# Turning round the operands of the state-space chunk products in a hybrid trunk kernel

## The reference

```
u = xc.reshape(B, L, 32, 16)
bu = einsum('blgc,gpc->blgp', u, b_bar)
states = scan(state_t = lam_bar * state_{t-1} + bu_t)
y = einsum('blgp,gcp->blgc', states, c).real + d_skip * u
y = gelu(y);  y = y * sigmoid(y @ glu_w + glu_b)
```

## Time and profile before

| | us |
|---|---|
| median of three runs | 1096.8 |
| profiled execution, time | 1097.05 |
| profiled execution, span | 1095.2 |
| PE busy | 915.2 (84% of the span) |
| PEld busy | 629.7 (57%) |
| DVE busy | 331.4 (30%) |
| ACT busy | 193.6 (18%) |
| POOL busy | 222.1 (20%) |
| mean granted TensorE clock | 0.91 |

### The profile page before, as it was taken

The page is one execution under the profiler, slowest core; times in us unless marked ns, Lnnn a source line. Parts: engine busy times, 40 slices in busy tenths (PEclk is TensorE's granted clock), DMA queues, the critical chain, the costliest instruction groups (busy, mean ns, idle before and its releaser), DMA issues.

```text
span 1095.2 us, 14939 instructions
## 1 busy us (share of the span) xinstructions
PE 915.2 (84%) x5341; PEld 629.7 (57%) x5342; DVE 331.4 (30%) x591; ACT 193.6 (18%) x282; POOL 222.1 (20%) x247
## 2 busy tenths in 40 slices
PE   3999898999999999984989878676995997787870
PEld 2788577888887688873555444433553554444430
DVE  2793995570042444445111101000110110010015
ACT  4523125130143223230000000000000000000002
POOL 3457970430110000011111110101201111111100
PEclk9999699985799999995999999987998999999895
DMA  8593120520343585220799999629997999999965
GB/s 240 107 180 97 39 77 20 105 94 0 83 148 97 185 335 180 88 80 19 294 405 411 395 398 402 274 61 402 406 386 282 407 395 398 412 405 408 407 252 234
DMA packets 80886, 263.02 MB, mean 240 GB/s; under 512 B 33323, under 2 KB 34347, under 8 KB 72130
## 3 DMA queue, kind: packets, MB, share of 16 engines
q1 hardware_dynamic: 74450, 252.00, 62.2%
q0 software_dynamic: 6256, 10.51, 2.8%
q10 hardware_dynamic: 144, 0.02, 0.0%
HBM read 256.07 MB, written 15.47 MB: 248 GB/s over the span
## 4 chain that ended last, share of the span: by engine, by line
PE 59%; DMA 26%; POOL 5%; DVE 4%; issue 2%; ACT 2%; SPq 1%; DVEq 0%; POOLq 0%; ACTq 0%
PE ps L911 27%; PE ps L422 13%; DMA au<-in_exp_w_up 13%; DMA ssm<-in_exp_w_up 8%; PE ps L435 7%; DMA pair<-h_scratch,idx_now 2%; DMA choice_rows<-pair,put_now 2%; PE ps L896 2%; PE ps L414 2%; PE ps L1014 2%; PE ps L1013 2%; POOL w_lo L1657 2%; POOL ssm L1667 2%; PE ps L1015 1%; PE ps L888 1%
## 5 line engine op out<-in xcount | busy, mean ns | idle before, releaser
L422 PE MATMUL ps<-ssm,pair 128*64 128x256 f32 x1696 | 196.3, 387 | 28.5 <-DMA ssm<-in_exp_w_gate 11.7
L422 PEld LDWEIGHTS ps<-ssm,pair 128*64 128x64 f32 x1696 | 124.1, 139 | 109.7 <-issue 31.6
L584 DVE TENSOR_TENSOR pair<-pair,ps 128x256 f32<-128x256 f32 x32 | 13.5, 421 | 404.2 <-PE ps L422 404.2
L911 PE MATMUL ps<-h_hi,w_hi 128*128 128x512 f32 x288 | 115.8, 402 | 7.9 <-POOL w_lo L1657 6.3
L911 PE MATMUL ps<-h_lo,w_hi 128*128 128x512 f32 x288 | 114.2, 397 | 0.0
L911 PE MATMUL ps<-h_hi,w_lo 128*128 128x512 f32 x288 | 114.1, 396 | 0.0
L1657 POOL TENSOR_TENSOR w_lo<-raw,w_hi 128x1024 fp32r<-128x1024 f32 x34 | 87.2, 2570 | 132.2 <-ACT w_hi L1089 131.9
L1089 ACT CAST w_hi<-raw 128x1024 fp32r<-128x1024 f32 x60 | 62.8, 1049 | 223.1 <-PE ps L911 222.6
L435 PE MATMUL ps<-ssm,pair 128*64 128x512 f32 x288 | 72.6, 650 | 17.6 <-DVE pair L593 12.2
L435 PE MATMUL ps<-hl,pair 128*64 128x512 f32 x272 | 69.6, 658 | 15.7 <-DVE pair L593 11.6
L650 ACT COPY late<-ps 128x512 f32<-128x512 f32 x32 | 18.8, 586 | 356.5 <-PE ps L435 356.5
(11 more groups left out here) (277 smaller groups left out, 1167.8 us busy)
## 6 DMA issues: line engine op xcount, KB each, us to landing
ssm<-in_exp_w_gate SPq DMA_DIRECT2D x32, 2048.0 KB
au<-in_exp_w_up SPq DMA_DIRECT2D x16, 2048.0 KB
ssm<-in_exp_w_up SPq DMA_DIRECT2D x16, 2048.0 KB
ssm<-in_exp_w_down SPq DMA_DIRECT2D x16, 2048.0 KB, 20.7
hl<-in_exp_w_down SPq DMA_DIRECT2D x16, 2048.0 KB, 23.0
raw<-in_w_in SPq DMA_DIRECT2D x40, 512.0 KB, 4.0
raw<-in_w_branch SPq DMA_DIRECT2D x12, 512.0 KB, 3.7
raw<-in_w_out SPq DMA_DIRECT2D x8, 512.0 KB, 8.1
```

Of the source, the lines that this page charges most:

```text
L422: t = nc.tensor.matmul(ps[CAP * h:CAP * (h + 1), bank, 0:HALF], xgT[b][:, k], w[:, k, HALF * h:HALF * (h + 1)], start=k == 0, stop=k == KD ...
L911: t = nc.tensor.matmul(bank, lhs, rhs, start=k == 0 and n == 0, stop=k == 2 * count - 1 and n == 2)
```

## The change

The chunk products exchange their operands. Now `u8v` and the states are stationary (64 columns: the chunks), and taps and carries move (128 columns: 8 tokens x 16 channels). The result has chunks on the partitions. Group q goes to partitions 0 to 63 and group q + 16 to partitions 64 to 127 of the same bank, and the two alternate in program order; for the carries their inputs also lie on the two halves of the partitions. ScalarE copies the banks out in another order of the elements (`y8w`). After `gate(2)`, TensorE turns the result back with 16 transpositions of 128x128 into four banks (`yt`), and VectorE reads them from PSUM when it adds `d_skip * u`. The DRAM scratch, its eight stores, its load and both waits of SyncE's queue are gone. The banks of all later steps of the dense part are exchanged, low for high. VectorE now makes unit 34 before, and not behind, the `d_skip` step, and that step's four parts come in the order 0, 2, 1, 3, as do the GELUs.

```
--- before.py
+++ after.py
@@ -91,13 +91,14 @@
     g += [(("bt", r, i), 4 + i) for r in range(2) for i in range(4)] + [(("k", i), i) for i in range(8)]
     g += [(("bu", h, r), 2 * h + r) for h in range(2) for r in range(2)] + four(("br", 0), high)
     g += four(("gt", 1), low) + four(("br", 1), high) + four(("y",), low)
-    g += four(("gt", 2), high) + four(("br", 2), low) + four(("gt", 3), high) + four(("br", 3), low) + four(("gl",), high)
+    g += four(("gt", 2), high) + four(("yt",), low) + four(("br", 2), high)
+    g += four(("gt", 3), low) + four(("br", 3), high) + four(("gl",), low)
     for n in range(4, len(GATE_STEPS)):
-        g += four(("gt", n), low) + four(("br", n), high)
-    g += four(("o", 0), low) + four(("o", 1), high)
+        g += four(("gt", n), high) + four(("br", n), low)
+    g += four(("o", 0), high) + four(("o", 1), low)
     for i in range(NT):
-        g += [(("rt", i, h), 2 * (i % 2) + h) for h in range(2)] + [(("lg", i), 4 + i)]
-    g += [("pos", 0), ("tok", 1)]
+        g += [(("rt", i, h), 4 + 2 * (i % 2) + h) for h in range(2)] + [(("lg", i), i)]
+    g += [("pos", 4), ("tok", 5)]
     uses, place = [0] * 8, {}
     for name, b in g:
         uses[b] += 1
@@ -132,7 +133,6 @@
 
 
     xc_d = nc.dram_tensor("xc_scratch", (W, T), F32, kind="Internal").ap()
-    y_d = nc.dram_tensor("y_scratch", (W, T), F32, kind="Internal").ap()
     h2_d = nc.dram_tensor("h2_scratch", (T, D), F32, kind="Internal").ap()
     res_d = nc.dram_tensor("choice_rows", (4 * T, W), F32, kind="Internal").ap()
 
@@ -230,7 +230,7 @@
         gluw = ssm[:, 0:2048].rearrange("p (k n) -> p k n", k=MW)
         btT = [early[:, Q * P * r:Q * P * (r + 1)].rearrange("p (q n) -> p q n", q=Q) for r in range(2)]
         u8v = u8.rearrange("p (g c) -> p g c", g=G)
-        y8v = y8.rearrange("p (g c) -> p g c", g=G)
+        y8w = y8.rearrange("p (m j q c) -> p m j q c", m=2, j=J, q=8)
         yT = u8.rearrange("p (m t) -> p m t", m=MW)
         st_re = st[:, 0:Q * NC].rearrange("p (q c) -> p q c", q=Q)
         st_im = st[:, Q * NC:2 * Q * NC].rearrange("p (q c) -> p q c", q=Q)
@@ -302,7 +302,7 @@
         w_hi_made, w_lo_pool, w_lo_dve, unit_used = (sem(n) for n in ("w_hi_made", "w_lo_by_pool", "w_lo_by_dve", "unit_used"))
         glu_in, router_in = sem("glu_in"), sem("router_in")
         x_again = sem("x_again")
-        xc_stored, u8_in, y_stored, yT_in, ker_in = (sem(n) for n in ("xc_stored", "u8_in", "y_stored", "yT_in", "ker_in"))
+        xc_stored, u8_in, ker_in = (sem(n) for n in ("xc_stored", "u8_in", "ker_in"))
         bank_full = [sem(f"bank_full{b}") for b in range(8)]
         bank_out = [sem(f"bank_out{b}") for b in range(8)]
         ident_ready, sgw_masked, ldt_spread, consts_made = (sem(n) for n in ("ident_ready", "sgw_masked", "ldt_spread", "consts_made"))
@@ -842,12 +842,7 @@
 
 
             taken(sp, ("y", MW - 1))
-            for j in range(J):
-                sp.dma_start(y_d.rearrange("(g c) (j n) -> j c g n", c=CH, j=J)[j],
-                             y8v[CH * j:CH * (j + 1)]).then_inc(y_stored, 16)
             sp.dma_start(gluw, glu_w[0].rearrange("(k p) n -> p k n", p=P)).then_inc(glu_in, 16)
-            sp.wait_ge(y_stored, 16 * J)
-            sp.dma_start(yT, y_d.rearrange("(m p) t -> p m t", p=P)).then_inc(yT_in, 16)
             load_units(36, 47)
 
 
@@ -1007,18 +1002,25 @@
             pe.wait_ge(st_ready, 1)
             for i in range(4):
                 bank = start(("y", i))
-                for g in range(8 * i, 8 * i + 8):
-                    rows, q = slice(S * (g // Q), S * (g // Q + 1)), g % Q
-                    o_ = bank[:, NC * (g % 8):NC * (g % 8 + 1)]
-                    nc.tensor.matmul(o_, toep[:, g], u8v[:, g], start=True, stop=False)
-                    nc.tensor.matmul(o_, cp_re[rows, q, 1:J + 1].rearrange("p j c -> p (j c)"), st_re[rows, q], start=False, stop=False)
-                    t = nc.tensor.matmul(o_, cp_im[rows, q, 1:J + 1].rearrange("p j c -> p (j c)"), st_im[rows, q], start=False, stop=True)
+                for q in range(4 * i, 4 * i + 4):
+                    outs = [bank[S * two:S * (two + 1), P * (q % 4):P * (q % 4 + 1)] for two in range(2)]
+                    halves = [slice(S * two, S * (two + 1)) for two in range(2)]
+                    for two in range(2):
+                        nc.tensor.matmul(outs[two], u8v[:, two * Q + q], toep[:, two * Q + q], start=True, stop=False)
+                    for two, rows in enumerate(halves):
+                        nc.tensor.matmul(outs[two], st_re[rows, q], cp_re[rows, q, 1:J + 1].rearrange("p j c -> p (j c)"), start=False, stop=False)
+                    for two, rows in enumerate(halves):
+                        t = nc.tensor.matmul(outs[two], st_im[rows, q], cp_im[rows, q, 1:J + 1].rearrange("p j c -> p (j c)"), start=False, stop=True)
                 end(("y", i), t)
 
-
-            for n in range(2, 4):
-                gate(n)
-                branch(n)
+            gate(2)
+
+            taken(pe, ("y", MW - 1))
+            for i in range(4):
+                turn(("yt", i), [y8w[:, i // 2, 4 * (i % 2) + j].rearrange("p q c -> p (q c)") for j in range(4)])
+            branch(2)
+            gate(3)
+            branch(3)
 
             pe.wait_ge(glu_in, 16)
             pe.wait_ge(yg_ready, MW)
@@ -1195,12 +1197,14 @@
             branch_hi(1)
             act.wait_ge(st_ready, 1)
             for i in range(4):
-                copy_out(("y", i), y8v[:, 8 * i:8 * i + 8].rearrange("p g c -> p (g c)"))
+                name = ("y", i)
+                nc.scalar.copy(y8w[:, i // 2, :, 4 * (i % 2):4 * (i % 2) + 4],
+                               full(act, name).rearrange("p (q j c) -> p j q c", q=4, j=J)).then_inc(out_of(name), 1)
             his(31, 34)
             gates(2)
             his(35, 36)
-            for m in range(MW):
-                act.wait_ge(ych_ready, m + 1)
+            for n, m in enumerate((0, 2, 1, 3)):
+                act.wait_ge(ych_ready, n + 1)
                 nc.scalar.activation(C[:, m].rearrange("p (c j) -> p c j", j=J),
                                      yT[:, m].rearrange("p (j c) -> p c j", j=J), ACT.Gelu_apprx_tanh).then_inc(yg_ready, 1)
             his(37, 40)
@@ -1468,10 +1472,19 @@
 
             merge(1)
             branch_lo(1)
-            v.wait_ge(yT_in, 16)
-            for m in range(MW):
-                vv.scalar_tensor_tensor(yT[:, m], C[:, m], cols[:, DSK + m:DSK + m + 1], yT[:, m], ALU.mult, ALU.add).then_inc(ych_ready, 1)
-            los(34, 36)
+            lo(34)
+            for i in range(4):
+                full(v, ("yt", i))
+            for m in range(2):
+                turned = ps[:, 2 * m:2 * m + 2].rearrange("p b (j two n) -> p two (b j) n", j=4, two=2)
+                for two in range(2):
+                    k = 2 * two + m
+                    vv.scalar_tensor_tensor(yT[:, k].rearrange("p (j n) -> p j n", j=J), C[:, k].rearrange("p (j n) -> p j n", j=J),
+                                            cols[:, DSK + k:DSK + k + 1], turned[:, two], ALU.mult, ALU.add).then_inc(ych_ready, 1)
+            v.wait_ge(ych_ready, MW)
+            for i in range(4):
+                v.sem_inc(out_of(("yt", i)), 1)
+            los(35, 36)
             merge(2)
             los(37, 42)
             merge(3)
```

## The result

The changed kernel has a median of 1060.8 us over four runs (1059.47 to 1062.01), the one before 1096.8 beside it: a ratio of 0.965, 95% interval 0.958 to 0.971. Forecast were 1063.0 us and 1057 to 1074. The profiled execution took 1059.47 us, with a span of 1057.7 us, so 37.5 us less span than before.

A forecast was written before the change was run, and what follows sets the result against it. TensorE was taken as the bound from 187.8 to 478 us, its chunk products slow by shape and clock. From 1097.05 us, 35.9 + 1.4 - 3.5 = 33.8 gained gave 1063.3 profiled, 1063.0 for the median; range 1057 to 1074.

The forecast's parts named there:

- The stage: Chunk products: 192 overlapping instructions, 10.5 us, plus 32 changes of input width, 4.5 us, together 15.0 instead of 50.9 us.
- The drain: Chunk products: each change of tiling mode also breaks an overlapping pair, 1.7 us more, making the stage 16.7 us.
- The clock: Chunk products: clock expected at 1.00 throughout, as in earlier gapless products that moved 128 columns from 174.2 to 186 us.
- The recovery behind it: The 288 unit products behind the chunk products: no clock to recover, 65.6 instead of 67.05 us, 1.4 us gained.
- The transpositions: Behind gate(2): 16 added at two instructions each, 3.5 us on TensorE's path at full clock.
- the step "cost 0" for the banks: Ahead of branch(2): TensorE's wait for the sigmoids is filled by the transpositions, cost 0; without them 1.5 us.
- The rule on transpositions and the clock: Behind gate(2): transpositions don't count as clock activity, so the clock falls; 3.5 + 1.4 us more, 1068 us; chance 0.10.
- The sum: Whole kernel: 35.9 gained in the chunk products, + 1.4 clock, - 3.5 transpositions = 33.8 us.
- The expert part: Behind the dense part: streams weights at its own pace, so taken as shifted, not stretched; first product about 34 us sooner.
- Halves that don't overlap: Chunk products: nothing overlaps, stage 25.4 us, 1073.4 us; if only the carries don't, 1070; chance 0.12.
- The lock-out: Chunk products: alternate halves each empty the array first, at half clock; stage 62 us, 1115 us; chance 0.02.
- A falling clock in the stage: Chunk products: clock falls all the same, the stage doubles to 30 us, 1079.4 us; chance 0.08.

The follow-up runs named there:

- taps first: Changed kernel with the taps of all groups ahead of all carries in the chunk products; four runs at 1069.7 to 1071.0 us, ratio to the kernel before 0.972.
- the kernel with four turns: Changed kernel with 4 of its 16 transpositions, one per bank, the other outputs not turned; three of four runs 1058.0 to 1060.4 us, the fourth 1074.88.
- both orders together: Changed kernel with all taps before carries and the products that make the taps on alternate halves; second set median 1053.05 us, ratio to the kernel before 0.956.
- halves apart: Against the kernel with taps before carries within each bank: each bank's upper-half products all before its lower; lowest run 1062.78 us, other three 1080.2 to 1081.9.

## Why the prediction was right, step by step

- **The stage.** Forecast 15.0, measured 15.32 us. Both terms hold by themselves: 0.056 us for overlapping halves (taps first), 0.15 to 0.16 us for a change of width (2, 8 and 32 changes). The doubt about the carries, which the trace of before never showed alternating, is settled by 128 of them in 7.13 us.
- **The drain.** With half a slot more per change the stage would have been 16.7 us. What I had read from the old stage, 0.14 a change, was all of it but 0.01 to 0.02; there was no half slot on top.
- **The clock.** It held, as the taps' products had suggested. But that row showed only half: the same products fail to bring a lost clock back. Of the 35.6 us that the stage became shorter, 20.5 are the clock: at 0.95 us a group the old stage would have taken 30.4 instead of 50.9 us. The remaining 15.1 are the shape. The split is counted in this order, the clock first.
- **The recovery behind it.** 288 products in 21.99 + 43.77 = 65.76 us instead of 67.05: 1.3 us, forecast 1.4.
- **The transpositions** were mis-sized, and their place as well. I gave each two instructions, as a product of plain float32 has; the row of 16 instructions that I priced from was 16 transpositions, not 8. They take 1.75 us, not 3.5. And the step "cost 0" for the banks was the wrong way round: with a quarter of the transpositions TensorE waits for the sigmoids until the same moment. The sum should have read 1.9 for the banks and nothing for turning.
- **The rule on transpositions and the clock** (the Trainium skill, TensorE: Matmul & The Clock Gate, Part 4) would have cost 4.9 us. No profile here shows such a fall: 1.00 at 270 to 275 us, and at 252 us with the transpositions straight behind the products, but each of these pieces is over in 2 us. More telling is the kernel with four turns: its clock came back at 172.7 us, after 4 us of idle and with nothing on the engine since 170.0 us but the earlier transpositions (the granted clock is 0.50 up to 172.5 us and 1.00 from 173.0). The same is seen at 174.3 and 174.4 us in the kernel with the transpositions ahead of the gate and in both profiles with both orders together.
- **The sum.** Dense part: 36.1 (stage, with 0.5 of an earlier start) + 1.3 - 1.9 = 35.5 measured, 33.8 forecast. Of the 1.7 between, 1.6 are the transpositions that cost less than was put down; the rest is an earlier start of the stage (0.5), which nobody forecast, against 0.3 for the stage and 0.1 for the recovery. The profiled execution was 3.8 us faster than forecast; the other 2 are from the expert part, and that they fell this way is luck. The expert part was taken as shifted. In the profiles it is 616.7 us (changed kernel) to 621.7 (halves apart), and 618.7 before the change. What moves it by these few microseconds stays open; no experiment aimed at it.
- **The rivals.** Halves that don't overlap: out, by the chain. The lock-out: out. A falling clock in the stage: out for the new shape, and shown for the old one in whatever order.

## What to carry to other kernels

Look at the granted clock stage by stage before counting instructions. Here a TensorE that was 100% busy stood at half clock with products that load 128 columns and move 64, and turning the operands round gained more by the clock (20.5 us) than by the work (15.1). Put products on different halves (of columns or of partitions) next to each other in program order, and keep products of one input width together. An operation that seems to stand on the path may only fill a wait that would be there without it: leave most of it out once and see.

## What the runs showed of the hardware

- A change of input width between products (128 to 64 partitions or back) costs 0.15 to 0.16 us at full clock where the halves overlap. For the old shape 0.14 was worked out from one group of six instructions.
- Products on the upper and the lower 64 partitions, which write the same 16 partitions of two banks, overlap fully: 128 in 7.09 us. So do products from the upper and the lower 64 partitions into the upper and the lower half of one bank: 128 in 7.13 us.
- The clock came back from 0.50 to 1.00 amid sixteen transpositions in four profiles; in that of the kernel with four turns at 172.7 us, with no other product on the engine for 8 us before. Sixteen of them in full-clock work (1.75 us) left it at 1.00.
- Gapless work of 128 columns loaded and 64 moved lost the clock (from 0.112 to 0.215 us an instruction). Gapless work of 16 loaded and 128 moved held 1.00 for 13.7 us where the clock had come back as it began, and stayed at 0.50 for 26.5 us where it had not; in the one profile of the same work in pairs that began low, it came back to 1.00 after 2 us.
- So one unchanged stage gave the kernel two times 13 us apart, before and after the change.
